# The last layer norm of a decoder step: normalised in feature-major tiles, or turned to rows first and normalised there

## The reference

```python
def _layernorm(x, g, b):
    mu = jnp.mean(xf, -1, keepdims=True)
    var = jnp.mean(jnp.square(xf - mu), -1, keepdims=True)
    return (xf - mu) * lax.rsqrt(var + LN_EPS) * g + b
...
f = jnp.square(jax.nn.relu(h2 @ p['w_up'])) @ p['w_down']
x = _layernorm(DEEPNORM_ALPHA * x + g2 * f, p['ln2_g'], p['ln2_b'])
```

## Time and profile before

| | |
|---|---|
| time, median of 3 runs | 1886.08 us (1882.89, 1886.08, 1889.31) |
| profiled execution, its own time | 1883.25 us |
| span, first to last instruction | 1881.8 us |
| PE busy | 1746.8 us, 93% |
| DVE busy | 1135.9 us, 60% |
| ACT, POOL busy | 294.6 us, 347.0 us |
| mean granted TensorE clock | 0.952 of full speed |

### The profile page before, as it was taken

How to read it: one execution, slowest core, us unless ns; L and a number is a source line. 1 busy time by engine, 2 the same in 40 slices (tenths; PEclk the granted TensorE clock), 3 DMA queues, 4 the chain that set the end, 5 groups by cost and what they waited for, 6 DMA issues and landing times.

```text
span 1881.8 us, 38998 instructions
## 1 busy us (share of the span) xinstructions
PE 1746.8 (93%) x15968; PEld 1541.5 (82%) x15968; DVE 1135.9 (60%) x1623; ACT 294.6 (16%) x726; POOL 347.0 (18%) x491
## 2 busy tenths in 40 slices
PE   4769999999999989998995999999999999999995
PEld 1349999776677556765994999999999999999994
DVE  0147777455445255446778676676666676667766
ACT  1030001333222224443003100000000000000003
POOL 0000100133333123533116220011000110011113
PEclk9779999999998889999997999999999999999996
DMA  9996553776655734554451545545545545545421
GB/s 326 339 310 218 178 175 111 266 241 238 236 175 179 249 117 129 157 180 162 135 172 53 175 152 167 178 151 165 179 152 163 173 148 172 172 142 180 152 73 51
DMA packets 285840, 333.52 MB, mean 177 GB/s; under 512 B 31962, under 2 KB 231162, under 8 KB 284986
## 3 DMA queue, kind: packets, MB, share of 16 engines
q1 hardware_dynamic: 281634, 324.27, 53.0%
q0 software_dynamic: 3072, 3.15, 0.6%
q10 hardware_dynamic: 978, 3.82, 0.6%
HBM read 323.63 MB, written 7.57 MB: 176 GB/s over the span
## 4 chain that ended last, share of the span: by engine, by line
PE 81%; DMA 6%; DVE 5%; issue 4%; POOLq 2%; ACT 1%; POOL 1%; SPq 0%; ACTq 0%; DVEq 0%
PE bank L1246 20%; PE bank L1248 20%; PE bank L1247 20%; DMA slab<-in_w_ada_dram 5%; PE bank L1304 3%; PE bank L1499 2%; DVE xT L2391 1%; POOLq L460 1%; PE bank L1205 1%; PE bank L1627 1%; PE bank L1486 1%; PE bank L1631 1%; PE bank L1217 1%; PE bank L1644 1%; PE bank L1194 1%
## 5 line engine op out<-in xcount | busy, mean ns | idle before, releaser
L1246 PE MATMUL bank<-arena_hi 128*128 128x288 f32 (+1 forms) x2816 | 836.2, 297 | 16.3 <-DVE hT_lo L1920 8.2
L1248 PE MATMUL bank<-arena_hi,slab_lo 128*128 128x288 f32 (+1 forms) x2816 | 829.2, 294 | 0.0
L1246 PEld LDWEIGHTS bank<-arena_hi 128*128 128x128 f32 (+1 forms) x2816 | 528.5, 188 | 18.7 <-issue 12.1
L1248 PEld LDWEIGHTS bank<-arena_hi,slab_lo 128*128 128x128 f32 (+1 forms) x2816 | 530.8, 189 | 0.0
L1247 PE MATMUL bank<-hT_lo,arena_hi 128*128 128x288 f32 (+2 forms) x1792 | 529.9, 296 | 0.0
L2328 DVE TENSOR_TENSOR slab_lo<-slab,arena_hi 128x2048 fp32r<-128x2048 f32 x144 | 351.3, 2440 | 4.9
L1247 PEld LDWEIGHTS bank<-hT_lo,arena_hi 128*128 128x128 f32 (+2 forms) x1792 | 337.5, 188 | 0.2
L2327 DVE CAST arena_hi<-slab 128x2048 fp32r<-128x2048 f32 x144 | 177.8, 1235 | 264.2 <-PE bank L1248 264.2
L1247 PE MATMUL bank<-arena_hi 128*128 128x288 f32 x1024 | 302.1, 295 | 0.0
L1247 PEld LDWEIGHTS bank<-arena_hi 128*128 128x128 f32 x1024 | 192.3, 188 | 0.0
L806 POOL TENSOR_TENSOR arena<-arena 128x288 f32<-128x288 f32 x64 | 67.2, 1051 | 640.2 <-ACT arena L1147 639.4
(11 more groups left out here) (370 smaller groups left out, 2006.4 us busy)
## 6 DMA issues: line engine op xcount, KB each, us to landing
slab<-in_w_ada_dram SPq DMA_DIRECT2D x48, 2048.0 KB, 9.0
slab<-in_w_up_dram SPq DMA_DIRECT2D x32, 2048.0 KB, 9.3
slab<-in_w_down_dram SPq DMA_DIRECT2D x32, 2048.0 KB, 8.2
slab<-in_w_in_dram SPq DMA_DIRECT2D x16, 2048.0 KB, 8.4
slab<-in_cache_latent_dram SPq DMA_DIRECT2D x128, 128.0 KB, 2.3
slab<-in_w_out_dram SPq DMA_DIRECT2D x8, 2048.0 KB, 8.7
xT<-in_cache_krope_dram POOLq DMA_DIRECT2D x96, 32.0 KB, 2.4
x_park<-xT SPq DMA_DIRECT2D x1, 2304.0 KB, 13.8
```

The source lines that it names most:

```text
L1246: pe.matmul(b[0:w, 0:NTOK], w_hi[:, k, 0:w], x_hi[:, k, :], start=(k == 0), stop=False)
L1248: mm = pe.matmul(b[0:w, 0:NTOK], w_lo[:, k, 0:w], x_hi[:, k, :], start=False, stop=(k == KT - 1))
```

## The change

- POOL builds 16 diagonal tiles `g_diag[k]` (the identity times the norm's scale for the 128 features of tile k), after its last relu square and ahead of `sum_tiles`.
- The blocks are turned before the norm is known, from `xT` as it is: for tokens t and features of tile k, a plain f32 matmul `xT[k]^T x g_diag[k]` gives the rows times the scale. Two of the eight prompt blocks come ahead of `ln_sums` on TensorE, six after it, then the sample block, whose four 512-column groups lie in four strips of 32 partitions of bank 7. ACT copies each block to `y_rows`, two of them before its root and seven after.
- `centre`, `scale_tile` and the affine step on `xT` are gone, and the 48 transposes with them.
- DVE makes `side`: in each strip of 32 partitions, row 0 is minus mean times reciprocal root (a value for each token), row 1 is ones. Small f32 matmuls turn the reciprocal root into columns (`rstd_col`, bank 4).
- Two small DMAs load scale and shift as rows `gb` (in each strip of 32 partitions row 0 is 512 values of the scale, row 1 of the shift). A matmul `side^T x gb` with two rows of contraction gives what has to be added to a block, in PSUM, in eight products and four for the sample block.
- DVE makes each block final in one instruction, rows times `rstd_col` plus the bank, nine of 128x512; SP stores as before, but the four sample parts all come last.

```diff
--- before.py
+++ after.py
@@ -359,6 +359,7 @@
         lnb, o = carve(o, 8, NTOK)
         relu, o = carve(o, 2, NTOK)
         relu_sq, o = carve(o, 2, NTOK)
+        assert o == 16768
         x_hi, o = carve(o, KT, NTOK, of=arena_hi)
         w_hi_a, o = carve(o, KT, P, of=arena_hi)
 
@@ -366,6 +367,11 @@
             early = {KT: w_hi_a, KT + 1: w_hi_b}
             return early[g] if isinstance(g, int) and g in early else w_hi[:, m % 2]
         y_rows, _ = carve(0, 3, D)
+        g_diag, _ = carve(16768 + KT * NTOK, KT, P)
+        gb, _ = carve(16768, 512)
+        side, rstd_col = lnb[:, 7, :], lnb[:, 4, 0:3]
+        Y_BLOCKS = [(t, g) for t in range(2) for g in range(4)]
+        RAW_BANKS, SHIFT_BANKS = (0, 1, 2, 3, 6), (0, 1, 2, 3, 5, 6, 7)
 
         ident = const[:, C_ID:C_ID + P]
         ones = const[:, C_ONE:C_ONE + P]
@@ -422,7 +428,7 @@
         win_split, hi_split = sem("win_split"), sem("hi_split")
         w_split, h_split, f_split, tile_mm, x_added = (sem(s) for s in ("w_split", "h_split", "f_split", "tile_mm", "x_added"))
         x_sq, x_acc1, x_acc2 = sem("x_sq"), sem("x_acc1"), sem("x_acc2")
-        ln_mm, ln_var, ln_std, ln_rstd, ln_cen, ln_nrm, ln_x = (sem("ln_" + s) for s in ("mm", "var", "std", "rstd", "cen", "nrm", "x"))
+        ln_mm, ln_var, ln_std, ln_rstd, ln_cen, ln_nrm, ln_side = (sem("ln_" + s) for s in ("mm", "var", "std", "rstd", "cen", "nrm", "side"))
         xa2_ready = sem("xa2_ready")
         up_relu, up_f = sem("up_relu"), sem("up_f")
         y_T, y_rows_a, y_rows_d = sem("y_T"), sem("y_rows_a"), sem("y_rows_d")
@@ -640,12 +646,17 @@
                     load(q * 4 + (4 + m // RING), m % RING,
                          w_dn[:, bass.ds(q, 1), :, m * SLAB_COLS:(m + 1) * SLAB_COLS].rearrange("p o k c -> p (o k) c"))
 
-            for n in range(12):
-                g, q = n // 3, n % 3
-                rows, cols = (P, slice(g * 512, (g + 1) * 512)) if q < 2 else (32, slice(g * 512, (g + 1) * 512))
-                sp.wait_ge(y_rows_a if n % 2 else y_rows_d, n // 2 + 1)
-                dst = a["y_prompt"][0, q * P:(q + 1) * P, cols] if q < 2 else a["y_sample"].rearrange("b t d -> (b t) d")[:, cols]
-                sp.dma_start(dst, y_rows[0:rows, q, cols]).then_inc(stored, 16)
+            sp.wait_ge(tile_mm, 8 * KT)
+            for n, name in enumerate(("ln2_g", "ln2_b")):
+                sp.dma_start(gb[n:P:32, :], a[name][0].rearrange("(g c) -> g c", g=4)).then_inc(uv_in, 16)
+            for n, (t, g) in enumerate(Y_BLOCKS):
+                sp.wait_ge(y_rows_d, n + 1)
+                cols = slice(g * 512, (g + 1) * 512)
+                sp.dma_start(a["y_prompt"][0, t * P:(t + 1) * P, cols], y_rows[:, t, cols]).then_inc(stored, 16)
+            sp.wait_ge(y_rows_d, 9)
+            for g in range(4):
+                sp.dma_start(a["y_sample"].rearrange("b t d -> (b t) d")[:, g * 512:(g + 1) * 512],
+                             y_rows[32 * g:32 * g + 32, 2, 0:512]).then_inc(stored, 16)
             sp.wait_ge(stored, 16 * (2 + 6 + 12))
         @block.gpsimd
         def _(pool):
@@ -809,9 +820,10 @@
             with pool.Fori(1, 4) as q:
                 for m in range(KT):
                     square(q, m)
+            for k in range(KT):
+                pool.tensor_scalar(g_diag[:, k, :], ident, par[:, P + 96 + k:P + 97 + k], None, ALU.mult).then_inc(ln_cen, 1)
             for n in range(KT):
                 sum_tiles(1, n)
-            centre(KT)
         @block.scalar
         def _(act):
 
@@ -1152,16 +1164,17 @@
                     up_copy(q, m)
             for n in range(KT):
                 squares(1, n)
+
+            def keep_rows(n):
+                act.wait_ge(y_T, n + 1)
+                t, g = Y_BLOCKS[n] if n < 8 else (2, 0)
+                b = bank[RAW_BANKS[n % 5]] if n < 8 else bank[7]
+                act.activation(y_rows[:, t, g * 512:(g + 1) * 512], b[:, :], ACT.Copy).then_inc(y_rows_a, 1)
+            for n in range(2):
+                keep_rows(n)
             norm(1)
-            for k in range(KT):
-                act.wait_ge(ln_nrm, KT + k + 1)
-                act.activation(xT[:, k, :], xT[:, k, :], ACT.Identity, scale=par[:, P + 96 + k:P + 97 + k],
-                               bias=par[:, P + 112 + k:P + 113 + k]).then_inc(ln_x, 1)
-            for n in range(1, 12, 2):
-                q = n % 3
-                rows = P if q < 2 else 32
-                act.wait_ge(y_T, n + 1)
-                act.activation(y_rows[0:rows, q, (n // 3) * 512:(n // 3 + 1) * 512], bank[n % 4][0:rows, :], ACT.Copy).then_inc(y_rows_a, 1)
+            for n in range(2, 9):
+                keep_rows(n)
         @block.tensor
         def _(pe):
 
@@ -1861,17 +1874,45 @@
             quarter(0, range(3, KT))
             with pe.Fori(1, 4) as q:
                 quarter(q, range(KT))
+            def raw_rows(n):
+                t, g = Y_BLOCKS[n]
+                b = bank[RAW_BANKS[n % 5]]
+                pe.wait_ge(x_added, 4 * KT + max(4 * g + 4, KT if n > 1 else KT - 2))
+                if n >= 5:
+                    pe.wait_ge(y_rows_a, n - 4)
+                for e in range(4):
+                    mm = pe.matmul(b[:, e * P:(e + 1) * P], xT[:, 4 * g + e, t * P:(t + 1) * P], g_diag[:, 4 * g + e, :], start=True, stop=True)
+                mm.then_inc(y_T, 1)
+            pe.wait_ge(ln_cen, 2 * KT)
+            for n in (0, 1):
+                raw_rows(n)
             ln_sums(1)
-
-            for n in range(12):
-                g, q = n // 3, n % 3
-                w = P if q < 2 else 32
-                pe.wait_ge(ln_x, 4 * g + 4)
-                if n >= 4:
-                    pe.wait_ge(y_rows_a if n % 2 else y_rows_d, (n - 4) // 2 + 1)
-                for e in range(4):
-                    tr = pe.transpose(bank[n % 4][0:w, e * P:(e + 1) * P], xT[:, 4 * g + e, q * P:q * P + w], ident)
-                tr.then_inc(y_T, 1)
+            for n in range(2, 8):
+                raw_rows(n)
+            for e in range(4):
+                for g in range(4):
+                    mm = pe.matmul(bank[7][32 * g:32 * g + 32, e * P:(e + 1) * P], xT[:, 4 * g + e, NP_TOK:NTOK], g_diag[:, 4 * g + e, :], start=True, stop=True)
+            mm.then_inc(y_T, 1)
+
+            pe.wait_ge(ln_rstd, 2)
+            for t in range(2):
+                pe.matmul(bank[4][:, t:t + 1], lnb[0:1, 3, t * P:(t + 1) * P], ones[0:1, 0:1], start=True, stop=True)
+            for g in range(4):
+                mm = pe.matmul(bank[4][32 * g:32 * g + 32, 2:3], lnb[0:1, 3, NP_TOK:NTOK], ones[0:1, 0:1], start=True, stop=True)
+            mm.then_inc(y_T, 1)
+            pe.wait_ge(y_rows_a, 9)
+            pe.wait_ge(ln_side, 1)
+            pe.wait_ge(uv_in, 48)
+            for n, (t, g) in enumerate(Y_BLOCKS):
+                if n >= 7:
+                    pe.wait_ge(y_rows_d, n - 6)
+                pe.matmul(bank[SHIFT_BANKS[n % 7]][:, :], side[32 * g:32 * g + 2, t * P:(t + 1) * P], gb[32 * g:32 * g + 2, :],
+                          start=True, stop=True).then_inc(y_T, 1)
+            pe.wait_ge(y_rows_d, 2)
+            for g in range(4):
+                mm = pe.matmul(bank[SHIFT_BANKS[1]][32 * g:32 * g + 32, :], side[32 * g:32 * g + 2, NP_TOK:NTOK], gb[32 * g:32 * g + 2, :],
+                               start=True, stop=True)
+            mm.then_inc(y_T, 1)
         @block.vector
         def _(dve):
             ch = Chain(dve, dve_step)
@@ -2432,13 +2473,17 @@
             quarter(3, True)
             add_square(1, KT - 1)
             norm(1)
-            for k in range(KT):
-                scale_tile(1, k)
-            for n in range(0, 12, 2):
-                q = n % 3
-                rows = P if q < 2 else 32
-                dve.wait_ge(y_T, n + 1)
-                dve.tensor_copy(y_rows[0:rows, q, (n // 3) * 512:(n // 3 + 1) * 512], bank[n % 4][0:rows, :]).then_inc(y_rows_d, 1)
+            ch.link(dve.scalar_tensor_tensor(lnb[:, 6, :], lnb[:, 2, :], -1.0, lnb[:, 3, :], ALU.mult, ALU.mult))
+            dve.tensor_scalar(side, lnb[:, 6, :], const[:, C_SEL:C_SEL + 1], const[:, C_SEL + 1:C_SEL + 2], ALU.mult, ALU.add).then_inc(ln_side, 1)
+            dve.wait_ge(y_T, 10)
+            ch.link(dve.tensor_copy(rstd_col, bank[4][:, 0:3]))
+            dve.wait_ge(y_rows_a, 9)
+            for n in range(9):
+                t, g = Y_BLOCKS[n] if n < 8 else (2, 0)
+                rows = y_rows[:, t, g * 512:(g + 1) * 512]
+                dve.wait_ge(y_T, 11 + n)
+                dve.scalar_tensor_tensor(rows, rows, rstd_col[:, t:t + 1], bank[SHIFT_BANKS[n % 7]][:, :], ALU.mult, ALU.add).then_inc(y_rows_d, 1)
+
 
 
 # ---- launch ----
```

## The result

The changed kernel takes 1872.74 us (median of 20 runs, 1864.75 to 1883.19), the kernel before 1881.0 us in the same series (20 runs, 1874.05 to 1890.38). The ratio, estimated over the runs, is 0.9946, with an interval of 0.9932 to 0.9961: 10.1 us less (7.3 to 12.8). The two medians by themselves lie 8.3 us apart. Forecast were 1874.0 us and 12.1 less.

A forecast was written before the change was run, and what follows sets the result against it. PE was busy 93% of the span, but the last 34 us were one serial chain. The terms ended the span at 1870.2 instead of 1881.8, 11.6 us less; 1886.08 - 11.6 = 1874.5, given as 1874, range 1867 to 1882.

The forecast's parts named there:

- Added work on POOL: Ahead of the tail: 16 diagonal tiles at up to 0.74 us, 0 to 11.8 us in all, hidden, costing nothing.
- the margin that was argued: POOL's sums: at 11.8 us of tiles the first comes 2.7 us late, hidden because the next is due 6.4 later.
- Two blocks in the hole: PE between last product and sums: two blocks take 2.0 us, sums start on time at clock 1.00, norm 0.9 us earlier.
- Norm 4.0: After the sums: the norm still takes 4.0 us, from 1850.85 to 1854.85.
- Turning, sample, columns: PE after the sums: six blocks 6.0 us, sample block 1.3, columns of the root 1.0.
- the lower end named: PE's turning: records 0.11 us apart instead of 0.125, making the six blocks 0.7 us less.
- First bank after 1.05, steps 0.67 apart, last 0.75: Last step: first shift bank at 1859.95, then DVE sets the pace with nine instructions, ending at 1866.05.
- Changes of form: PE's tiling mode changes four times in the tail: nothing by the earlier trace, at most 1.2 us by the skill's rule.
- Stores, 4.15 us behind DVE's last step: End of the tail: 0.1 + 3 x 0.46 + 2.69 us after 1866.05, so the span ends at 1870.2.
- The charge of 1.4 for four sample stores at the end: End of the tail: four sample stores come last instead of one store, costing 1.4 us of what is won.
- Clock 1.00 in the windows after 1850: Sign that the forecast is right: PE no longer stands idle in the tail, so its clock stays at 1.00.
- The slower rival: Last step: clock drops and shift products run in a row, 1.9 us each; execution 1891.7 us, 8.4 slower; chance 0.06.

The follow-up runs named there:

- added work: Kernel before plus only POOL's 16 diagonal tiles and the two loads of scale and shift, which nothing uses: 1883.54 us against 1882.47, ratio 1.002.
- no block ahead: Changed kernel with no block turned ahead of the sums, all eight after them on PE: 1873.4 us.
- the second interleaved run: Second profile of the changed kernel with sample block and four shift products ahead of the last two raw blocks, ACT issuing the sample stores: 1872.71 us.
- the run with the turning behind the norm: Changed kernel with blocks 2 to 7 waiting for the root, PE kept busy meanwhile by 16 matmuls that nobody reads: 1876.48 us.
- the run in one strip: Changed kernel with all shift products in the first strip of 32 rows instead of going round four: 1877.99 us.
- the interleaved runs without the stalled issue: Changed kernel, sample and four shift products ahead of the last two raw blocks: second profile with ACT issuing sample stores, 1872.71 us; SP issuing all, 1874.14 us.
- full clock on the transposes: Kernel before with matmuls that nobody reads put in holes where PE had been waiting in the tail: 1890.68 us.
- The interleaved order: Changed kernel with sample block and four shift products ahead of the last two raw blocks; ACT issuing sample stores 1872.56 us, SP issuing all 1874.14 us.

## Why the prediction was right, step by step

The forecast tail was 1870.2 - 1847.8 = 22.4 us, the measured one is 20.96. That the time came within 1.3 us of the 1874.0 is in part luck: the forecast started from the 1886.08 of three runs of before, which twenty put at 1881.0, and the gain came out at 10.1 us (7.3 to 12.8) where 12.1 were forecast. By its steps:

- *Added work on POOL:* size wrong (17.7 us for 0 to 11.8), conclusion right. The bound came from a product of two tensors with twice the columns at 0.74 in the earlier trace rows; the group of the same operation, shown above, would have been the nearer row. The first sum came 8.6 us late (T0 - 83.0 instead of T0 - 91.6), more than the 6.4 to the next one, so the margin that was argued did not hold; the sums had caught up by the fourth: 101.64 us to T0 in all three kernels.
- *Two blocks in the hole, 2.0 us; sums on time, at full clock; norm at T0 + 3.06:* 1.95, and T0 + 3.16. Right. The reason given, that the clock stays at 1.00, holds; of three traces with PE idle at this place, the clock fell 0.3 us into the sums in one (before, T0 + 2.2), and when they were nearly through in the others (added work, T0 + 3.0; no block ahead, T0 + 3.1).
- *Norm 4.0:* 4.0.
- *Turning, sample, columns, 6.0 + 1.3 + 1.0:* 5.45, 1.01 and 0.79, each from its start to the next one's. The turning began at T0 + 2.96 instead of 2.71; together the shift begins at T0 + 10.21 instead of 11.1. This is the largest of the mis-sized terms: a record lies 0.1135 after the one before it, at the lower end named, not 0.125.
- *First bank after 1.05, steps 0.67 apart, last 0.75:* 1.27, 0.66, 0.75. In one strip a bank took 0.83 at full clock, so four take 3.3; in four strips the four products of the second interleaved run, which no bank holds up, take 1.14, 2.9 times less:

```profile
1859.60 1.14 PE L1915 MATMUL bank<-arena 2*128 2x512 f32 x8
```

  The Trainium skill, "TensorE: Matmul & The Clock Gate", section on packing small matmuls by row and column tiling, gives 3.07 for four strips; the trace agrees closely.
- *Changes of form, nothing by the earlier trace rows:* not quite nothing. The reading went by modelled ends of records, and by those the rows here look alike (1861.75 before 1856.30 + 5.52). From start to start the first record in strips comes 0.205 us after the last full-size one, where full-size ones lie 0.11 apart; the change from strips to single rows takes 0.203. The earlier trace rows has the same step, 0.203 against 0.109. So a change costs about 0.1 us, at most some 0.4 for all four, which the measured terms above contain.
- *Stores, 4.15 us behind DVE's last step:* 3.46 (1870.84 to 1874.3). The issues lay 0.46 apart as forecast; the last one needed 2.1 and not 2.69. The charge of 1.4 for four sample stores at the end was wrong as a mechanism: with half of them on a second queue only 0.3 came back of the 0.9 expected, and the blocks' own bytes keep the DMA engines at 375 GB/s or more from 1867 to 1872.

Together, with 0.1 less ahead of the shift: 0.25 - 0.55 - 0.29 - 0.21 - 0.1 + 0.22 - 0.09 - 0.69 = -1.46 us, the difference of the two tails (22.41 and 20.96).

"Clock 1.00 in the windows after 1850" failed from 1866 on. It fell in PE's stretch of two-row products, and it cost nothing: in the run with the turning behind the norm DVE's nine steps lie 0.66 apart over products at 0.50 from 1866 on. The slower rival needed both, the drop and products in a row; the run in one strip has the drop halfway and, behind it, the 1.7 us a bank that it named as 1.9.

What the prediction did not draw from its own terms is how much of the tail the stores hold. It had a block stored in 0.75 us, about DVE's pace. From the first store's issue to the end it is 8.7 us after, 8.4 with two queues, 8.7 both with no block ahead and behind the norm, 9.4 in the interleaved runs without the stalled issue, and 8.95 in the old order with the added work. Two megabytes and a third at 380 GB/s (375 to 387 in the windows from 1867 to 1872) is 6.2 of them. That this is a floor, which a faster last step could not pass, is argued: no run had a faster last step. The first store moved from T0 + 24.4 to T0 + 12.25, and that is 12.2 of the 13.05 us.

## What to carry to other kernels

In a tail that ends in stores, look first at when the first store is issued and how long the bytes take from there: what brings the first store forward counts (12.2 us earlier, 13.05 won), and a faster step behind it can give nothing, as full clock on the transposes showed (2.2 us less work, nothing won). The interleaved order shows the share that is left: first store 1.9 us earlier, DVE's last step 1.4, and 1.2 won, or 0.4 where an issue stalled. A norm that is linear in what is known late (a factor and an offset for each row) can have its layout change ahead of it; here a third of the gain (4.4 of 13.05) came from that overlap, and most of the rest came with the passes that were dropped. For the cost of a new operation take a row of the same operation and engine, even of another size, before one of another operation at the nearer size.

## What the runs showed of the hardware

- POOL's multiplication by a column took 1.1 us for 128x128 (16 in 17.69), as long as a multiplication and addition by columns for 128x288 (1.08).
- PE's clock fell to 0.50 while PE showed as busy with products of two rows (after: 0.71 in 1866 to 1867, 0.50 behind it). In the run in one strip it fell too (0.52 in 1865 to 1866), where these records had followed each other 0.43 us apart with no wait for a bank. And behind the same idle hole it fell at about T0 + 2.2 in the trace of before and T0 + 3.0 with the added work.
- Going from full-size products to strips, and from strips to single rows, took 0.205 and 0.203 us from start to start (after, 1861.55 to 1861.75 and 1862.56 to 1862.76), where two full-size records lie 0.11 apart: about 0.1 us a change. The Trainium skill, "TensorEngine Tiling (Array Packing)", Key Properties, has a change of tiling mode drain the engine; the trace agrees as far as there is a cost, and puts it at these 0.1 us.
